# Attention layers behind a mixture of experts: two heads' queries and keys to a unit, scores spread over the units, keys first, three modulation units moved to TensorE

## The reference

```python
# second layer, first half: differential attention, 8 heads, two maps of 64 for each
q, k, v = jnp.split(h @ w_qkv, 3, axis=-1)            # 1024 each
q = rope on the first 16 of every 64 channels, times 64 ** -0.5;  k likewise
p = softmax(q k^T) for both maps;  w = p[0] - lam * p[1]
o = rmsnorm(w @ v, subln_g) * (1 - lam_init);  y = o @ w_o
# third layer, first half: 8 query heads on 2 key heads of 128
q = rope(rmsnorm(q, qnorm_g)), k = rope(rmsnorm(k, knorm_g))   # over all 128 channels
y = (softmax(q k^T * 128 ** -0.5) @ v) @ w_o
# second half of both: (silu(gate) * up) @ w_out with gate, up = split(h @ w_in)
```

## Time and profile before

| | us |
|---|---|
| median of 3 runs (lowest to highest) | 1319.41 (1317.56 to 1320.39) |
| the profiled execution | 1320.98 |
| its span on the core | 1319.2 |
| PE busy | 1123.8 (85%) |
| DVE busy | 674.1 (51%) |
| ACT busy | 545.1 (41%) |

### The profile page before, as it was taken

The page is one execution under the profiler, slowest core; times in us unless marked ns, Lnnn a source line. Parts: engine busy times, 40 slices in busy tenths (PEclk is TensorE's granted clock), DMA queues, the critical chain, the costliest instruction groups (busy, mean ns, idle before and its releaser), DMA issues.

```text
span 1319.2 us, 19883 instructions
## 1 busy us (share of the span) xinstructions
PE 1123.8 (85%) x8439; PEld 845.6 (64%) x8439; DVE 674.1 (51%) x1415; ACT 545.1 (41%) x1185; POOL 0.2 (0%) x4
## 2 busy tenths in 40 slices
PE   6999999867666675757799889999999979999997
PEld 5777667534333442424467667788887758788886
DVE  4575665111111010101077776898886865777765
ACT  4554554111111111101155654666644754666653
POOL 0000000000000000000000000000000000000000
PEclk9999999989897988889899989999999999999999
DMA  9996947999999999999997416686757613655500
GB/s 388 424 425 250 391 158 296 429 426 427 427 426 428 423 427 428 427 427 426 427 390 297 192 64 238 267 320 251 310 209 297 247 64 132 251 192 192 192 32 32
DMA packets 29702, 397.36 MB, mean 301 GB/s; under 512 B 3496, under 2 KB 4904, under 8 KB 5416
## 3 DMA queue, kind: packets, MB, share of 16 engines
q1 hardware_dynamic: 29176, 395.72, 73.3%
q10 hardware_dynamic: 432, 0.30, 0.1%
HBM read 394.97 MB, written 1.05 MB: 300 GB/s over the span
## 4 chain that ended last, share of the span: by engine, by line
PE 55%; DMA 23%; DVE 13%; ACT 7%; issue 1%; DVEq 0%; ACTq 0%
PE ps L1161 16%; DMA ring<-in_w13b 12%; PE ps L1165 8%; DMA mem<-in_w13b 6%; PE ps L1155 5%; PE ps L1157 4%; PE ps L1156 4%; ACT mem L1863 4%; DVE memr L2364 4%; PE ps L1691 4%; DMA ring<-in_w13a 3%; ACT memr L1863 3%; DVE mem L2364 2%; PE ps L1651 2%; PE ps L1195 2%; PE ps L1746 2%
## 5 line engine op out<-in xcount | busy, mean ns | idle before, releaser
L2364 DVE TENSOR_TENSOR memr<-ring,memr 128x512 fp32r<-128x512 f32 x432 | 292.0, 689 | 166.1 <-ACT memr L1863 162.8
L1863 ACT ACTIVATE memr<-ring 128x512 fp32r<-128x512 f32 x432 | 264.5, 628 | 176.9 <-PE ps L1157 67.7
L1863 ACT ACTIVATE mem<-ps 128x512 f32<-128x512 f32 (+5 forms) x307 | 128.2, 438 | 393.5 <-PE ps L1691 236.7
L1161 PE MATMUL ps<-memr 128*128 128x512 f32 x1056 | 275.3, 394 | 3.4 <-DVE memr L2364 2.1
L1161 PEld LDWEIGHTS ps<-memr 128*128 128x128 f32 x1056 | 186.7, 189 | 36.5 <-DVE memr L2370 5.1
L1155 PE MATMUL ps<-memr 128*128 128x256 f32 (+2 forms) x504 | 180.1, 357 | 6.6 <-DVE memr L2364 4.1
L2364 DVE TENSOR_TENSOR mem<-mem,ps 128x512 f32<-128x512 f32 (+1 forms) x76 | 43.5, 572 | 248.1 <-ACT mem L1863 248.0
L1156 PE MATMUL ps<-memr 128*128 128x256 f32 (+2 forms) x504 | 165.9, 329 | 0.0
L1157 PE MATMUL ps<-memr 128*128 128x256 f32 (+2 forms) x504 | 165.8, 329 | 0.0
L1165 PEld LDWEIGHTS ps<-memr 128*128 128x128 f32 x1056 | 151.4, 190 | 16.5 <-DVE memr L2370 0.9
L1165 PE MATMUL ps<-memr 128*128 128x256 f32 x1056 | 156.9, 282 | 0.9 <-DVE memr L2370 0.5
(11 more groups left out here) (180 smaller groups left out, 1039.7 us busy)
## 6 DMA issues: line engine op xcount, KB each, us to landing
ring<-in_wpk SPq DMA_DIRECT2D x89, 2048.0 KB, 9.7
ring<-in_w13a SPq DMA_DIRECT2D x17, 2048.0 KB, 44.8
mem<-in_w13b SPq DMA_DIRECT2D x16, 2048.0 KB, 45.8
ring<-in_w SPq DMA_DIRECT2D x16, 2048.0 KB, 45.2
ring<-in_w13b SPq DMA_DIRECT2D x16, 2048.0 KB, 42.9
mem<-in_w13a SPq DMA_DIRECT2D x15, 2048.0 KB, 45.4
mem<-in_w SPq DMA_DIRECT2D x15, 2048.0 KB, 45.6
mem<-in_wpk SPq DMA_DIRECT2D x1, 2048.0 KB, 10.4
```

The source lines that it names most:

```text
L1161: return self.e.matmul(ps[:, 0:512], a[0], b[1], start=start, stop=stop)
L1863: return self.e.activation(out, src, f, **k)
L2364: return self.e.tensor_tensor(out, a, b, op)
```

## The change

In the second layer a unit now holds the queries and the keys of two heads. `qk0` to `qk3` come first and then the two units of values. A unit's queries and keys are transposed after slabs 3 and 4 of the next unit; ACT copies the queries (and scales them, which rope did before), DVE the keys. All scores, weights and turns are one sequence of 18 steps, a step every second slab from the second unit on; values and endings are another, which begins in the second unit of values and ends in the output product. The turned weights have a slot for each head. The three ada units that DVE did in this layer become matmuls on PE.

In the third layer keys and values come first. The first queries' rope takes two steps a slab during the second queries' slabs 1 to 4, and their transposes come behind slab 4; the first three steps of the heads come at slabs 6 to 8. In the stretch behind, the second queries' rope takes two steps for each step of the heads.

```diff
-       ((1, 4), (1, 5), (1, 6)), ((1, 11), (2, 0), (2, 1)),
+       ((1, 4), (1, 5), (1, 6), (1, 7)), ((1, 8), (1, 9)), ((1, 11), (2, 0), (2, 1)),
-TURNED_1 = ((1, 7), (1, 8), (1, 9))
-        self.qst1 = [span(10240 + 1024 * j, 2, 512) for j in range(3)]
-        self.e21, self.e2T1 = span(13312, 4, 2, 256), span(15360, 2, 2, 256)
+        self.qst1 = [span(10240 + 1024 * j, 2, 512) for j in range(2)]
+        self.e21 = span(13312, 4, 2, 256)
+        self.e2T1 = [span(o + 512 * j, 2, 256) for o in (15360, 12288, 10240, 11264) for j in range(2)]
...
+    def turn_both(self, tag, src, ready, g):
+
+        yield
+        yield
+        self.turn_pair(tag, 0, src, ready, self.m.qT1[:, 2 * g:2 * g + 2, :], 0.125, self.a_free)
+        yield
+        self.turn_pair(tag, 2, src, ready, self.m.kT1[:, 2 * g:2 * g + 2, :], 1.0, self.a_free)
+        yield
...
+    def scores_pair(self):
+
+        for step in range(18):
+            if step < 16 and step % 2 == 0:
+                self.a_scores(1, step // 2)
+            if 1 <= step < 17:
+                self.a_weigh(1, step - 1)
+            if 2 <= step:
+                self.a_turn(1, step - 2)
+            yield
+
+    def values_pair(self):
+
+        for h in range(0, 8, 4):
+            for n in range(5):
+                if n:
+                    self.a_end(1, h + n - 1)
+                if n < 4:
+                    self.a_values(1, h + n)
+                yield
...
-    def layer2(self, at):
+    def layer2(self):
-        self.slow = self.turned_units(TURNED_1, 5)
-        qk_unit("q10", 0, 0.125, m.qT1, 0, self.a_free)
+        qk_unit(0)
+        self.side.append(self.paced(self.scores_pair(), [5] + [1] * 17))
+        self.side.append(self.paced(self.values_pair(), [32, 1, 0, 1, 0, 1, 1, 1, 1, 0]))
         self.ada_unit(1, 5)
-        qk_unit("k10", 1, 1.0, m.kT1, 0, self.a_free)
+        qk_unit(1)
         self.ada_unit(1, 6)
+        qk_unit(2)
+        self.ada_unit(1, 7)
+        qk_unit(3)
         v_unit(0)
-        self.side.append(self.paced(at, [1] * 8))
-        qk_unit("q11", 2, 0.125, m.qT1, 1, self.a_free)
-        qk_unit("k11", 0, 1.0, m.kT1, 1, self.turned("q10"))
-        self.side.append(self.paced(at, [4, 0, 0, 0]))
+        self.ada_unit(1, 8)
         v_unit(1)
...
-        self.side.append(self.paced(at, [0] * 9))
...
     def layer3(self, at):
+        self.project("kv2", m.h2, low)
+        self.copy_kv()
+        self.side.append(self.chain(*[rope("kv2", m.kvb[:, tt, 0:256], 2, 1, tt, tt) for tt in range(2)],
+                                    self.turn("kv2", m.kvb, [(s.dve_att, ("nr", "kv2", 1))], m.kT2, n=2, free=self.a_free)))
         self.project("q20", m.h2, low)
         self.copy_q("q20", m.qst2[0])
-        self.side.append(self.chain(*[rope("q20", m.qst2[0][:, tt, :], 4, 0, tt, tt) for tt in range(2)]))
-        self.project("kv2", m.h2, low)
-        self.copy_kv()
         self.drain()
...
+        first_q = self.chain(*[rope("q20", m.qst2[0][:, tt, :], 4, 0, tt, 2 + tt) for tt in range(2)],
+                             self.turn("q20", m.qst2[0], [(s.dve_att, ("nr", "q20", 1))], m.qT2[:, 0:4, :], free=self.a_free))
+        self.side += [first_q, first_q]
+        self.side.append(self.paced(at, [5, 0, 0]))
         self.project("q21", m.h2, low)
...
-        for step in range(12):
+        for step in range(3, 12):
...
             next(at)
             next(last_q, None)
+            next(last_q, None)
```

More of the change, by code:

```diff
@@ L737, in turn, with turn_on_act @@
         for c2 in range(0, n, 2):
-            self.turn_pair(tag, c2, src, ready, dst, scale, free)
+            self.turn_pair(tag, c2, src, ready, dst[:, c2:c2 + 2, :], scale, free)
             yield
+    def turn_both(self, tag, src, ready, g):
[5 more added lines that the diff above has]
+        yield
+    def turn_on_act(self, tag, c2, scale):
+        return c2 == 0 if tag[:2] == "qk" else c2 % 4 or scale != 1.0
     def turned(self, tag, n=4, scale=1.0):
-        on_act = lambda c2: c2 % 4 or scale != 1.0
-        return [(self.s.act_att if on_act(c2) else self.s.dve_att, ("turn", tag, c2)) for c2 in range(0, n, 2)]
+        return [(self.s.act_att if self.turn_on_act(tag, c2, scale) else self.s.dve_att, ("turn", tag, c2))
+                for c2 in range(0, n, 2)]
     def attention_first(self):
@@ L882, in second_norm_part, with qk_unit @@
         yield
-    def layer2(self, at):
+    def layer2(self):
         m, s = self.m, self.s
         low = lambda k: (s.dve_h, ("low", (1, 0), k))
-        def qk_unit(tag, slot, scale, dst, g, free):
+        def qk_unit(g):
+            tag, store = f"qk{g}", m.qst1[g % 2]
             self.project(tag, m.h2, low)
-            self.rope1(tag, m.qst1[slot], scale, free)
-            self.side.append(self.turn(tag, m.qst1[slot], [(s.dve_att, ("rope", tag, 1))], dst[:, 4 * g:4 * g + 4, :], waits=2,
-                                       free=self.a_free))
+            self.rope1(tag, store, 1.0, self.a_free if g < 2 else self.turned(f"qk{g - 2}"))
+            self.side.append(self.turn_both(tag, store, [(s.dve_att, ("rope", tag, 1))], g))
         def v_unit(g):
@@ L923, in layer3 @@
         rope = lambda tag, buf, nh, qk, tt, j: self.norm_rope(tag, buf, nh, qk, tt, j)
+        self.project("kv2", m.h2, low)
+        self.copy_kv()
+        self.side.append(self.chain(*[rope("kv2", m.kvb[:, tt, 0:256], 2, 1, tt, tt) for tt in range(2)],
+                                    self.turn("kv2", m.kvb, [(s.dve_att, ("nr", "kv2", 1))], m.kT2, n=2, free=self.a_free)))
         self.project("q20", m.h2, low)
         self.copy_q("q20", m.qst2[0])
-        self.side.append(self.chain(*[rope("q20", m.qst2[0][:, tt, :], 4, 0, tt, tt) for tt in range(2)]))
-        self.project("kv2", m.h2, low)
-        self.copy_kv()
         self.drain()
-        self.side.append(self.turn("q20", m.qst2[0], [(s.dve_att, ("nr", "q20", 1))], m.qT2[:, 0:4, :], free=self.a_free))
-        self.side.append(self.chain(*[rope("kv2", m.kvb[:, tt, 0:256], 2, 1, tt, 2 + tt) for tt in range(2)],
-                                    self.turn("kv2", m.kvb, [(s.dve_att, ("nr", "kv2", 1))], m.kT2, waits=2, n=2, free=self.a_free)))
+        first_q = self.chain(*[rope("q20", m.qst2[0][:, tt, :], 4, 0, tt, 2 + tt) for tt in range(2)],
+                             self.turn("q20", m.qst2[0], [(s.dve_att, ("nr", "q20", 1))], m.qT2[:, 0:4, :], free=self.a_free))
+        self.side += [first_q, first_q]
+        self.side.append(self.paced(at, [5, 0, 0]))
         self.project("q21", m.h2, low)
@@ L1059, in stages @@
     for i in (1, 2):
-        at = p.attention(i)
+        at = p.attention_last() if i == 2 else iter(())
         if i == 1:
-            p.layer2(at)
+            p.layer2()
         else:
@@ L1084, in stages @@
         if i == 1:
[L1085 removed]
+            p.slow = p.turned_units(TURNED, 4)
         for n in range(11):
@@ L1470, in turn_pair @@
         r.then_inc(*s.pe_att.up(("turn", tag, c2)))
-        self.give(("turn", tag, c2), (s.act_att if c2 % 4 or scale != 1.0 else s.dve_att, ("turn", tag, c2)))
+        self.give(("turn", tag, c2), (s.act_att if self.turn_on_act(tag, c2, scale) else s.dve_att, ("turn", tag, c2)))
     def a0_scores(self, h):
@@ L1536, in a_scores @@
         if i == 1:
-            ready = self.turned(f"q1{h // 4}") + self.turned(f"k1{h // 4}")
+            ready = self.turned(f"qk{h // 2}")
         else:
@@ L2186, in a_turn @@
         h, tt = j // 2, j % 2
[L2187 removed]
+        eT = m.e2T1[h] if i == 1 else m.e2T2[:, h % 2]
         w.wait_ge(s.pe_att, ("e", i, j))
[L2189 removed]
+        if i == 2 and h >= 2:
             w.wait_ge(s.pe_att, ("v", i, h - 2))
[L2191 removed]
+        self.act(eT[:, :, 128 * tt:128 * tt + 128], m.of(("e", i, j))[:, 0:256].rearrange("p (c n) -> p c n", c=2)
                  ).then_inc(*s.act_att.up(("e", i, j)))
@@ L2671, in turn_pair @@
         w, s, m = self.w, self.s, self.m
-        if not c2 % 4 and scale == 1.0:
+        if not self.turn_on_act(tag, c2, scale):
             w.wait_ge(s.pe_att, ("turn", tag, c2))
```

50 lines of the change are left out of this document (21 added, 29 removed).

## The result

| | us |
|---|---|
| before, median of 6 (in later series 1319.9 to 1320.6) | 1319.84 |
| changed, median of 6 | 1325.56 (1320.82 to 1326.44) |
| ratio, 95% interval | 1.004 [1.003, 1.005] |
| the same kernel in another series, 11 runs | 1325.09, ratio 1.0032 [1.0021, 1.0042] |
| first profiled execution (span 1319.0) | 1320.82 |

The change makes the kernel slower by some 4 to 6 us. The forecast was 1318.9 and "no change"; the time lies inside the range, at its upper end, beside the times of rivals 1 (1324.8) and 4 (1325.5). The first profile is of the fastest of six executions, so a second one stands beside it.

What follows compares the result with a forecast made beforehand. It took PE's waits on DVE and ACT in the second layer as the bound there. Second layer -7 plus third +6.5 gave -0.5 us against the profiled 1320.98, carried to the 1319.41 median as 1318.9; range 1310 to 1326.

Steps and rivals of the forecast that it cites:

- rival 1: Third layer's wait also halves the clock (1.7 us), half the second layer's turns still wait (4.2): 1324.8 us, chance 0.18.
- Rival 4: Moved units add 6.3 us to PE, DVE's free time goes unused, second layer gains 0: 1325.5 us, chance 0.08.
- The second layer, -7: Second layer's net change: 11 us still lost plus 6.3 more PE work minus 24, -6.7, stated as -7 us.
- 11 us of lost time: Second layer: waits at the first units, key copies, turns and endings, plus one clock fall, expected to remain: 11 us.
- the 24 that I took off: Second layer before: 15.1 us of PE idle, 5.4 of reduced clock, 3.5 of tails at waits, together 24 us.
- the 6.3 that I put on: Second layer: three units moved to PE, four more transposes and three more changes of work add 6.3 us.
- its wait at 680.28: Second layer's first unit: delay of the split behind 680.28 goes with DVE's piece at 680.05; 2.0 of 3.0 us stays.
- 1.9 and 4.6: Third layer: PE waits 1.9 us for the keys' turn and 4.6 us for the first queries' turn.
- +6.5: Third layer's net change: 2.3 for the keys' turn, 5.4 for the second queries' unit, -1.4 back: +6.3, stated +6.5 us.
- the +9 that I had set as its bound with the clock: Third layer's upper bound: 9 us slower if the wait also costs clock.
- Rival 2: Third layer costs only about +3 us, its stretch before the scores of head 4 shrinking to 13: 1315.4 us, chance 0.17.
- Rival 3: Second layer's waits vanish nearly all, 6 us left in place of 11: sum -5.5, 1313.9 us, chance 0.17.

Runs made afterwards that it cites:

- e7: The second layer's new order with the third layer as before, but its three ada units back on DVE (against e2): 1320.74 us, ratio to before 1.0008.
- e11: Changed kernel with extra transposes keeping PE busy in the third layer's wait for the first queries' turn and ahead of its first six turns of weights: 1321.13 us.
- e3: The kernel before with only the third layer's change, second layer as before: 1332.26 us, ratio to before 1.0091.
- e1: The changed kernel run again without edits, for its intervals and a second profile: 1325.09 us, ratio to before 1.0032.
- e2: The second layer as changed, with the third layer as before: 1314.52 us, ratio to before 0.9959.
- e6: Changed kernel with 44 overwritten transposes keeping PE busy in the third layer's wait for the first queries' turn: 1322.79 us, ratio to before 1.0024.

## Why the prediction was wrong

- **The second layer, -7 forecast, -7.1 measured.** The sum was right by luck, for its parts were not. I kept 11 us of lost time; counted in the same way 8.9 are left (7.2 of PE's 128.47 idle, no loss of clock, 0.16 at each of 11 waits), which would make the layer 8.8 shorter. So the 24 that I took off was too much, or the 6.3 that I put on too little, by 1.7; the rows don't tell which. The parts, with what is left in brackets: turns of weights 1.75 (0.7), copies of keys 1.55 (2.6), endings and the output unit 4.2 (1.0 for the sums of squares, 0.4 for values), a fall of the clock 1.0 (none). Of the first unit I said that its wait at 680.28 goes with the piece on DVE; it stayed, 1.2 in place of 1.16, so the piece wasn't its cause. That the waits come with the three units on DVE is shown by e7.
- **The waits of the third layer.** 1.9 and 4.6 forecast, 1.78 and 4.77 measured, both ended by DVE's rope. The whole without the clock was +6.5; e11 shows +6.7.
- **The step that failed: the clock was priced at nothing in the sum.** I had the row for it (a mean clock of 0.66 behind 3 us with 1.13 of PE), put 1.7 on it and left it to rival 1. A wait of 4.8 with nothing on PE is emptier than the stretch of that row, so by the row the fall was the likely case. It came in both profiles of the changed kernel and in e3's, and cost 1.6 and 2.3 us in the former. A second came 17 to 24 us later, of which no rival spoke, and cost 0 and 2.6. Together they cost 1.65 and 4.9 of the layer, and 3.7 in the median. The third layer alone is 11.6 over before in the median (e3), beyond the +9 that I had set as its bound with the clock. The Trainium skill's rule stood beside the row: an idle array is throttled ("TensorE: Matmul & The Clock Gate", Part 1). The trace agrees: the granted clock was 0.50 from within the wait (second profile) or from its end (first profile) on.
- **The sum of the layers.** -7 + 6.5 would have been a fair forecast of the kernel of e11 (0.8 over before, 95% interval -0.1 to +2.2). In e1's profile -7.1 for the second layer, +6.7 for the waits and +4.9 for the clock make +4.5, which is what e1's median is over before.
- **Rivals.** Rival 1 had the right sign and half of the mechanism: the clock, at 1.7 where it cost 3.7. Its other half, turns of the second layer that keep their waits, didn't happen, so that its 1324.8 came close by luck. Rival 2 is refuted: the stretch from the second queries' end to the scores of head 4 shrank by 1.2 (17.7 to 16.5, from 1060.3 to 1076.78), not to 13. Rival 3's second layer, 12 us shorter, didn't come: it was 7.1, and scores still waited 2.6 for the copies of the keys. Rival 4, whose time (1325.5) is the nearest to the measured one, is refuted by e2 and nearly turned round by e7: the moved units were the gain.

## What to carry to other kernels

A transpose that PE reaches before its producer stops every ready slab behind it (4.77 us here); count the producer's queue from the event that starts it, and put the turn behind as many slabs as that takes. Then price a wait twice: its length, and what runs at half clock behind it, and look whether PE-bound work stands there. And read more than one profile where a sum depends on the clock: here two of one kernel differ by 3.2 us in one layer.

## What the hardware showed that I had not expected

The clock fell not only behind an empty PE but behind a stretch where PE was busy for more than half of the time (9.29 of the 16 us ahead of the four with the fall, in e6). Where a fall began, how long it lasted and whether it met work that PE sets the pace of changed from execution to execution at unchanged waits: 67.35 and 70.57 us for one layer of one kernel. And work without use on PE made a kernel faster: 0.8 over before (e11) in place of 4.5.
